# Spreading the modulation loads differently between the weight loads of a fused two-block transformer kernel

## The reference

```
mod = silu(c) @ w_ada + b_ada                    # w_ada is 2048 x 12288, 96 MB
sh1, sc1, gt1, sh2, sc2, gt2 = split(mod, 6)
h    = rms_norm(x) * (1 + sc1) + sh1
proj = h @ w_in                                  # q, k, v of 8 heads, then the latents cq, ckv, k_pe
a    = differential_attention(q, k, v)           # 8 heads
q_m  = rms_norm(cq)  @ w_q_b                     # the latent projections
kv   = rms_norm(ckv) @ w_kv_b
b    = latent_attention(q_m, kv, k_pe)           # 8 heads
x    = x + gt1 * ([a, b] @ w_out)
h2   = rms_norm(x) * (1 + sc2) + sh2
x    = x + gt2 * ((silu(h2 @ w_gate) * (h2 @ w_up)) @ w_down)
```

## Time and profile before

| | us |
|---|---|
| three executions | 2655.3, 2654.34, 2660.18 |
| the profiled execution: its own time | 2656.51 |
| its span (first to last instruction) | 2654.1 |
| PE busy | 2583.4 (97%) |
| DVE busy | 1547.0 (58%) |
| ACT busy | 1166.7 (44%) |
| bytes from and to memory | 563.80 MB, 212 GB/s over the span |

### The profile page before, as it was taken

How to read it: one execution, slowest core, us unless ns; L and a number is a source line. 1 busy time by engine, 2 the same in 40 slices (tenths; PEclk the granted TensorE clock), 3 DMA queues, 4 the chain that set the end, 5 groups by cost and what they waited for, 6 DMA issues and landing times.

```text
span 2654.1 us, 32740 instructions
## 1 busy us (share of the span) xinstructions
PE 2583.4 (97%) x12054; PEld 2074.6 (78%) x12054; DVE 1547.0 (58%) x1698; ACT 1166.7 (44%) x1522; POOL 54.3 (2%) x86
## 2 busy tenths in 40 slices
PE   7999989899999999999999999999999999999997
PEld 2676766688888888887888888888888888888886
DVE  1456664577776555557655454566555656555555
ACT  2344554344444444444544455444544444444443
POOL 1010110000000000000000000000000000000000
PEclk8999999899999999999999999999999999999999
DMA  9968776657776555555655545566555555555552
GB/s 391 384 231 292 261 270 239 229 199 248 250 249 222 191 191 190 191 191 178 211 191 186 177 153 175 186 202 238 188 193 189 190 190 190 190 190 189 188 189 98
DMA packets 263106, 563.80 MB, mean 212 GB/s; under 512 B 9251, under 2 KB 13525, under 8 KB 261869
## 3 DMA queue, kind: packets, MB, share of 16 engines
q1 hardware_dynamic: 260688, 549.25, 61.0%
q0 software_dynamic: 1952, 11.27, 1.2%
q10 hardware_dynamic: 380, 2.13, 0.2%
HBM read 558.40 MB, written 4.21 MB: 212 GB/s over the span
## 4 chain that ended last, share of the span: by engine, by line
PE 83%; DVE 2%; ACT 1%; issue 0%; DMA 0%; POOL 0%; DVEq 0%; POOLq 0%; ACTq 0%
PE acc L635 79%; PE bank L716 2%; PE bank L665 1%; DVE w_lo L1681 0%; PE acc L857 0%; PE acc L909 0%; PE bank L728 0%; PE bank L866 0%; PE acc L855 0%; DMA raw<-in_w_ada 0%; DVE wide L2191 0%; DVE x_res L2195 0%; PE acc L1067 0%; PE acc L1068 0%; DVE actT_hi L1812 0%
## 5 line engine op out<-in xcount | busy, mean ns | idle before, releaser
L1681 DVE TENSOR_TENSOR w_lo<-raw,w_hi 128x1024 fp32r<-128x1024 f32 x852 | 1037.7, 1224 | 831.1 <-ACT w_hi L1153 802.3
L1153 ACT ACTIVATE w_hi<-raw 128x1024 fp32r<-128x1024 f32 x852 | 902.8, 1062 | 1059.0 <-PE acc L635 948.8
L635 PE MATMUL acc<-w_hi,actT_hi 128*128 128x512 f32 (+1 forms) x2112 | 833.7, 395 | 2.0 <-DVE actT_lo L1814 0.8
L635 PE MATMUL acc<-w_hi,actT_lo 128*128 128x512 f32 (+1 forms) x2112 | 821.8, 389 | 0.0
L635 PE MATMUL acc<-w_lo,actT_hi 128*128 128x512 f32 (+1 forms) x2112 | 821.4, 389 | 0.0
L635 PE MATMUL acc<-w_hi,mixT_hi 128*128 128x512 f32 (+1 forms) x1280 | 504.1, 394 | 9.6 <-DVE mixT_lo L1804 5.4
L635 PE MATMUL acc<-w_hi,mixT_lo 128*128 128x512 f32 (+1 forms) x1280 | 497.6, 389 | 0.0
L635 PE MATMUL acc<-w_lo,mixT_hi 128*128 128x512 f32 (+1 forms) x1280 | 497.2, 388 | 0.0
L635 PEld LDWEIGHTS acc<-w_hi,actT_hi 128*128 128x128 f32 x2112 | 397.6, 188 | 108.5 <-issue 21.7
L635 PEld LDWEIGHTS acc<-w_hi,actT_lo 128*128 128x128 f32 x2112 | 397.4, 188 | 82.6
L635 PEld LDWEIGHTS acc<-w_lo,actT_hi 128*128 128x128 f32 x2112 | 397.8, 188 | 79.6 <-issue 1.0
(11 more groups left out here) (275 smaller groups left out, 1066.9 us busy)
## 6 DMA issues: line engine op xcount, KB each, us to landing
raw<-in_w_ff SPq DMA_DIRECT2D x128, 1024.0 KB, 5.1
raw<-in_w_in SPq DMA_DIRECT2D x108, 1024.0 KB, 5.2
raw<-in_w_ada SPq DMA_DIRECT2D x64, 1024.0 KB, 5.2
raw<-in_w_gate SPq DMA_DIRECT2D x44, 1024.0 KB, 5.1
raw<-in_w_up SPq DMA_DIRECT2D x44, 1024.0 KB, 5.1
raw<-in_w_down SPq DMA_DIRECT2D x44, 1024.0 KB, 5.0
early_mix<-in_w_ada SPq DMA_DIRECT2D x16, 1024.0 KB, 8.8
wide<-in_w_ada SPq DMA_DIRECT2D x16, 1024.0 KB, 8.7
```

Of the source, the lines that this page charges most:

```text
L635: last_mm = pe.matmul(acc[p][:, t, 0:width], act[x][:, k0 + c, t * P:(t + 1) * P], w[:, u % SPL, c * NW:c * NW + width], start=first and c ...
L1153: act.activation(w_hi[:, u % SPL, :], raw[:, ld % RAW, (u % DU) * 1024:(u % DU + 1) * 1024], ACT.Copy) \
L1681: dve.tensor_tensor(w_lo[:, u % SPL, :], raw[:, ld % RAW, (u % DU) * 1024:(u % DU + 1) * 1024], w_hi[:, u % SPL, :].bitcast(F32), ALU.subt ...
```

## The change

The table of the gaps is another one. Before, 24 pairs are spread evenly over 39 weight loads (13 to 51), which puts nine of them one load behind the pair before. Now a pair stands behind every second load from 12 to 30, behind every load from 32 to 40, and behind every second load from 42 to 50. The bytes, the instructions and their number are the same; their order differs.

```diff
-GAPS = [0] * 12 + [2 * ((i + 1) * 24 // 39 - i * 24 // 39) for i in range(39)] + [0] * 3
+GAPS = [0] * 12 + [2, 0] * 10 + [2] * 8 + [2, 0] * 6 + [0] * 2
 ORDER = "".join("w" + "a" * g for g in GAPS)
 assert len(GAPS) == 54 and sum(GAPS) == 80 - NPRO
```

## The result

The change makes the kernel slower: 2668.05 us (median of six, 2667.26 to 2674.28) against 2656.53 us for the kernel before (2654.34 to 2660.18). The ratio is 1.0046, with a 95% interval of 1.0034 to 1.0057. I had forecast 2653.2 us. The profiled execution took 2674.28 us, the highest of the six, so what is read from its trace lies above what the median shows (17.8 us more than the profiled execution before, against 11.5 in the medians). Sizes of causes are therefore taken from the timed ratios further down, as far as their intervals allow; the trace says where they stand.

A forecast was written before the change was run, and what follows sets the result against it. PE, busy 97% of the span, was taken as the bound, so order only changes its idle time. Outside -12.1 us plus the run +9.95 gave -2.1: 2654.4, or 2653.2 us as a median; range 2646 to 2662.

The forecast's parts named there:

- All waits for modulation loads outside go too ... What is late next there I take as nothing.: Outside loads 32 to 40: 4.7 us of PE waits vanish and no later wait replaces them.
- Sign (1): From 160 us to pair 32: no modulation-load wait above 0.3 us; unit 62 ends about 7 us earlier, near 303.
- 32 to 33: Run step from the end of pair 32 to that of 33: the ring's loop decides, 10.2 us.
- 33 to 34: Run step from the end of pair 33 to that of 34: PE's own work and the pair, 9.7 us.
- 36 to 37: Run step from the end of pair 36 to that of 37: a chain through ACT and POOL, 11.4 us.
- 34 to 35: Run step between ends of pairs 34 and 35: late DVE sum, landing and second half, 13.5 us.
- Pair 40 costs its 1.85 in full.: Last pair of the run: distances exceed the ring's loop, so it adds only its own 1.85 us.
- sign (4): Behind pair 40: lag against the kernel before shrinks from about +3 to -2 us by unit 107.
- Sign (2): From the end of unit 62 to unit 75: about 66 us, with idle time of 13 to 14.
- sign (3): Line 665's longest wait is at pair 35, 3 to 5 us, for a load issued after a late DVE sum.
- The transfers become the bound: Rival for loads 32 to 40: each step 11.1 us, plus lower clock; together +5.5, 2661 us; chance 0.17.
- The gaps are filled: Rival for 310 to 368 us: extra pairs fit PE's idle time, run costs 8.1 less, 2645 us; chance 0.30.

The follow-up runs named there:

- The three repairs: Changed kernel with pair 30 moved to 29, pair 32 to 31, and the load of x issued later; all together 2655.03 us, ratio 0.9992.
- f4: Kernel before with pair 29 alone moved to 30; 2661.93 us, ratio 1.0017.
- e8: Kernel before with its pairs up to 31 at every odd load from 9, and pair 34 moved to load 10; 2662.58 us, ratio 1.0020.
- e1: Changed kernel with pair 30 alone moved to 29; 2664.64 us, ratio 1.0026.
- f3: Changed kernel in which the two loads of pair 33 alone bring 256 KB each instead of 1 MB; 2664.96 us, ratio 1.0030.
- f2: Changed kernel with pair 32 alone moved to 31; 2663.61 us, ratio 1.0027.
- x later: The 2 MB load of x on POOL's queue held back behind a later pair's sum; alone in the changed kernel 2667.43 us, ratio 1.0032.
- e5: Changed kernel with pairs 30 and 32 moved to 29 and 31; 2660.80 us, ratio 1.0011.
- e6: Changed kernel with pairs 30 and 32 moved to 29 and 31 and the load of x issued later; 2655.03 us, ratio 0.9992.
- e4: Changed kernel in which the modulation loads of pairs 32 to 40 bring 256 KB each instead of 1 MB; 2658.51 us, ratio 0.9996.
- e2: Kernel before up to pair 31, then pairs behind every load from 33 to 40, and 43, 45, 47, 50; 2663.55 us, ratio 1.0019.
- e3: Changed kernel with the load of x held back until the sum of pair 42; 2667.43 us, ratio 1.0032.
- e7: Kernel before with its first twelve pairs at every odd load from 9 to 31; 2655.57 us, ratio 0.9992.
- f1: Kernel before with the load of x issued only after the sum of pair 42; 2656.64 us, ratio 0.9998.

## Why the prediction was wrong, step by step

In terms of lag, the prediction was -7.0 us at unit 62, +8.1 for the run, +1.85 for pair 40, -5.1 behind it. The trace has -1.2, +16.5, +6.5 and -5.7. Only the last held. The three misses sum to 18.9 us in that execution. In the timed ratio the change costs 12.2 us where -2.1 was forecast, 14.3 us off. The three repairs take back as much, but a repair is not the same thing as a miss: moving pair 32 changes only the entry into the run.

- **"All waits for modulation loads outside go too ... What is late next there I take as nothing."** The first half held: no wait for a load above 0.3 us from 160 us to pair 32, and -7.1 us at unit 57, just as worked out. The second half failed. Pair 29 with its own wait of 1.13 us had kept PE behind the softmax chain of a head; without it the transposes come 1.29 us too early. And pair 30 now stands right behind these transposes and needs the bank that DVE has to empty (2.63 us). f4 reproduces both waits in the kernel before; e8 shows that the second belongs to the place, as a column step pays it too, with pair 29 there. Price: 5.8 us of lag, and 5.3 in the ratios of e1. Sign (1), unit 62 ending near 303, came out as 309.82.
- **"32 to 33 ... value 10.2."** It took 14.1 (311.67 to 325.77). All three terms were too small: the lag of the sum 4.6 against 2.9, the landing 7.5 against 6.3, the second half 2.0 against 1.0, as it ran at the lower clock. The measured neighbour behind the upper bound, pair 34 before, already had a landing of 7.7 in its 11.1; what it did not have is so late a sum (2.3 there) and the lower clock. f3 and f2 show from two sides that the loop at this place is the price.
- **The clock had no term in the sum.** "33 to 34", "35 to 36" and "36 to 37" took 11.7, 9.4 and 12.9 against 9.7, 8.5 and 11.4, together 4.4 us more. The work was counted at the full clock, and unit 65 (4.05 against 2.35), unit 69 (3.38 against 2.33) and pair 37 (3.37 against 1.92) ran in part at the lower one: 1.7 + 1.05 + 1.45 = 4.2 of the 4.4. With 1.0 in the step from 32 to 33, the lower clock is some 5 of the 8.4 us by which the run was missed, by this account of one trace. The prediction had it only in a rival, with 1.7 us.
- **"34 to 35: the critical one ... Value 13.5."** 13.6 (337.47 to 351.11). The lag of the sum was 6.7 against 7.3, the landing 4.9 against 5.2, the second half 2.0 against 1.0, again at the lower clock. The bank that I had called ready was not: 2.22 us for `q_nope`. But the second load came at 349.13 in any case, so that wait did not set the end. "37 to 38" held (10.7).
- **"Pair 40 costs its 1.85 in full."** I looked at PE's distance to pair 39 and at the loop, and not at what else moves then. POOL's loads were in the trace before, at 377 us, where no pair needed a load soon. The wait of 3.14 us and the lower clock behind it (unit 79 took 5.05 us instead of 3.02) make 8.1 us from unit 76 to 80 instead of 1.85. From unit 75 on it is 6.5, as in the trace before unit 75 itself ran at the lower clock. x later gives 5.0 us back in the ratios of e5 and e6.
- **The sum itself.** The parts named for four of the steps add up to 9.6, 8.25, 11.25 and 10.55 and were entered as 9.7, 8.5, 11.4 and 10.7. That is 0.65 us in all, and changes nothing in the argument. The 4.4 us for a landing, which stood beside the sum, are by a formula that the Trainium skill, "DMA: Bandwidth & Descriptors", section "Anatomy of one DMA", gives for the path of GpSimd. The modulation loads come by SyncE's queue, and none from 300 to 412 us landed in less than 4.8 us.
- **Behind the run**, -5.1 forecast, -5.7 measured, so the lag shrinks from unit 80 to 107 as sign (4) had it, though from +21.9 and not from +3. Sign (2), 66 us, came out as 74.25, past the 70 at which I had said it would be wrong; sign (3) missed, as the longest wait for a load stands at pair 40.

*The rivals.* "The transfers become the bound" gave 2661 us and was nearest. The mean step came out as 12.1 us, past the 11.9 from which it was to decide, the lower clock came with it, and e4 shows that the bytes are the price. But it is not the mean rate that binds, as the rival had it: the run moved 255 GB/s, less than the 282 of before in the earlier trace rows. Single landings decide, between stretches with nothing in flight. "The gaps are filled" failed for the change as made, but e6 gives it some right: with the entry mended, the stretch from unit 62 to 75 costs only 5.2 us for two pairs more (3.7 of work). What stays open is why the changed kernel's profiled execution lies 6 us over its median. Of this, 2.4 us arise at one unit near 1250 us, outside this stage, in a spell of the lower clock; the traces of e1, e2, e3 and e6 have the same spell and those of the others do not, so it does not belong to the change.

The best of these kernels, e6 at 2655.03 and e7 at 2655.57 us, cannot be told from the kernel before.

## What to carry to other kernels

Where loads pass through a ring in order, ask of each step not only when the one load may be issued, but what is released together with it: a stretch with nothing in flight, then several loads issued at once, is the mark of a ring that is given back late. Price a wait of 2 to 3 us on PE twice, as itself and, in some executions, as work at the lower clock around it. Before moving an item away from a place, look at which chain it was covering there; before putting one in a place, look at which buffer it takes and who filled that last. And list the transfers of every queue over the stretch, not only those of the queue that is reordered.

## What the runs showed of the hardware

A load of 768 KB took 9.1 us from issue to landing behind two of 1 MB, and 4.7 us behind two of 256 KB. A 1 MB load beside 2 MB of another queue took 11.6 us, the median in the kernel being 5.3.

TensorE fell to 1.2 GHz around short waits: two of 2.50 and 2.28 us with 2 us of matmuls between them put 320 to 328 us at a clock of 0.50, and in f4, behind waits of 1.30 and 2.63 us, the pair at 296.47 took 3.64 us instead of 1.92. The wait of 2.8 us ahead of pair 37 was followed by the lower clock in the changed kernel and in f1, and not in the kernel before nor in e6. The Trainium skill, "TensorE: Matmul & The Clock Gate", section "HAM oscillation — how this bites in real kernels", describes waits for data that send the array back to the lower clock again and again. The trace agrees for pairs 33 and 40, which waited for loads; of the five spells in this stage (one before) the other three came with waits for other engines' work.
